# RWKV's group norm inside the recurrence, its output projection entered by halves, and the feed-forward's sums by halves

## The reference, cut to what matters

```python
def swiglu(x, w_in, w_out):
    gate, up = jnp.split(x @ w_in, 2, axis=-1)
    return (jax.nn.silu(gate) * up) @ w_out
# RWKV, after the scan over the tokens has given y (16 heads of 64)
    mean = jnp.mean(y, axis=-1, keepdims=True)
    var = jnp.mean(jnp.square(y - mean), axis=-1, keepdims=True)
    y = ((y - mean) * lax.rsqrt(var + RWKV_LNX_EPS)).reshape(bsz, seq, D_MODEL)
    y = y * lnx_g.astype(f32) + lnx_b.astype(f32)
    bonus = jnp.sum(r_h * k_h * r_k.astype(f32), axis=-1, keepdims=True) * v_h
    y = y + bonus.reshape(bsz, seq, D_MODEL)
    return (y * g.astype(f32)).astype(x.dtype) @ w_o
```

## Time and profile before

| | |
|---|---|
| median of 3 runs | 3061.42 us (3059.08 to 3068.48) |
| the profiled execution | 3060.07 us, its span 3058.2 us |
| mean granted TensorE clock | 0.987 of full |
| TensorE, VectorE, ScalarE, GpSimd busy | 95%, 68%, 46%, 2% |
| recurrence | about 1376 to 1583.5 us |
| from its end to the output projection's first matmul | 1583.5 to 1617 us |
| output projection | 1617 to 1641.8 us |
| moved from and to memory | 471 MB, 154 GB/s over the span |

### The profile page before, as it was taken

The page is one execution under the profiler, slowest core; times in us unless marked ns, Lnnn a source line. Parts: engine busy times, 40 slices in busy tenths (PEclk is TensorE's granted clock), DMA queues, the critical chain, the costliest instruction groups (busy, mean ns, idle before and its releaser), DMA issues.

```text
span 3058.2 us, 43817 instructions
## 1 busy us (share of the span) xinstructions
PE 2915.9 (95%) x17418; PEld 2526.0 (83%) x17418; DVE 2077.7 (68%) x2566; ACT 1420.9 (46%) x1778; POOL 48.5 (2%) x43
## 2 busy tenths in 40 slices
PE   7998999999999999999999999998999999989998
PEld 6887787888888788888977888886887888988887
DVE  5767677776767677677766767766776775565676
ACT  4445545445444544652214445445545444445443
POOL 0000000000000000100000000000000000000000
PEclk9999999999999999999999999999999999999999
DMA  8643565654466566440004665643565656643662
GB/s 234 203 117 125 178 199 154 192 174 126 137 186 192 164 187 176 127 143 3 1 23 145 192 185 166 206 132 115 177 192 160 191 163 179 187 135 123 201 192 83
DMA packets 614845, 471.23 MB, mean 154 GB/s; under 512 B 40545, under 2 KB 572385, under 8 KB 614708
## 3 DMA queue, kind: packets, MB, share of 16 engines
q1 hardware_dynamic: 614084, 467.60, 50.6%
q10 hardware_dynamic: 624, 1.71, 0.2%
HBM read 466.37 MB, written 1.84 MB: 153 GB/s over the span
## 4 chain that ended last, share of the span: by engine, by line
PE 80%; DVE 10%; ACT 6%; issue 2%; DMA 0%; PEldq 0%; SPq 0%; PEld 0%; DVEq 0%; ACTq 0%
PE pair_bank L402 25%; PE pair_bank L403 13%; PE pair_bank L577 11%; PE out_banks L422 6%; PE out_banks L424 6%; PE out_banks L423 6%; DVE low L337 3%; ACT high L333 2%; PE out_banks L577 2%; PE pair_bank L2168 2%; PE pair_bank L2182 1%; PE pair_bank L2180 1%; DVE h L720 1%; DVE y L710 1%; DVE sq_scratch L484 0%
## 5 line engine op out<-in xcount | busy, mean ns | idle before, releaser
L337 DVE TENSOR_TENSOR low<-raw,high 128x3072 fp32r<-128x3072 f32 (+2 forms) x328 | 934.4, 2849 | 589.0 <-ACT high L333 588.2
L402 PE MATMUL pair_bank<-x_parts,high 128*128 128x512 f32 x3520 | 1240.9, 394 | 26.8 <-DVE x_parts L777 21.6
L403 PE MATMUL pair_bank<-x_parts,low 128*128 128x256 f32 x3520 | 985.7, 280 | 0.0
L333 ACT ACTIVATE high<-raw 128x3072 fp32r<-128x3072 f32 (+2 forms) x328 | 774.0, 2360 | 150.2 <-PE out_banks L424 51.7
L402 PEld LDWEIGHTS pair_bank<-x_parts,high 128*128 128x128 f32 x3520 | 661.1, 188 | 185.6 <-issue 27.3
L403 PEld LDWEIGHTS pair_bank<-x_parts,low 128*128 128x128 f32 x3520 | 666.1, 189 | 9.1
L452 ACT ACTIVATE sq_scratch<-pair_bank 128x512 f32<-128x512 f32 x220 | 132.0, 600 | 541.8 <-PE pair_bank L403 541.8
L422 PE MATMUL out_banks<-high,hid_h 128*128 128x512 f32 x880 | 348.2, 396 | 11.4 <-DVE hid_l L493 11.4
L424 PE MATMUL out_banks<-high,hid_l 128*128 128x512 f32 x880 | 347.8, 395 | 0.0
L423 PE MATMUL out_banks<-low,hid_h 128*128 128x512 f32 x880 | 347.7, 395 | 0.0
L454 ACT ACTIVATE silu<-sq_scratch 128x256 f32<-128x256 f32 x220 | 91.9, 418 | 351.7 <-DVE sq_scratch L484 351.7
(11 more groups left out here) (363 smaller groups left out, 3115.8 us busy)
## 6 DMA issues: line engine op xcount, KB each, us to landing
raw<-in_ffn_w_in_dram SPq DMA_DIRECT2D x352, 512.0 KB
raw<-in_ffn_w_out_dram SPq DMA_DIRECT2D x176, 512.0 KB
raw<-in_ffn_w_dram SPq DMA_DIRECT2D x132, 512.0 KB
raw<-in_w_in_dram SPq DMA_DIRECT2D x32, 1024.0 KB
raw<-in_gla_w_in_dram SPq DMA_DIRECT2D x12, 1024.0 KB
raw<-in_rwkv_w_rkv_dram SPq DMA_DIRECT2D x12, 1024.0 KB
raw<-in_swa_w_qkv_dram SPq DMA_DIRECT2D x10, 1024.0 KB
raw<-in_swa_w_o_dram SPq DMA_DIRECT2D x8, 1024.0 KB
```

The source lines that it names most:

```text
L333: nc.scalar.activation(high[u % SPLIT][:, lo:w], raw[u % RAW][:, lo:w], ACT.Copy).then_inc(high_ready, count)
L337: nc.vector.tensor_tensor(low[u % SPLIT][:, lo:w], raw[u % RAW][:, lo:w], high[u % SPLIT][:, lo:w].bitcast(F32), ALU.subtract).then_inc(we ...
L402: nc.tensor.matmul(o, H[:, w], x_parts[:, k, :], start=(k == 0), stop=False)
L403: last = nc.tensor.matmul(o[:, 0:SEQ], L[:, w], xh[:, k, :], start=False, stop=(k == KB - 1))
```

## The change

Seven parts, all in one diff:

- **Group norm in the recurrence.** The two tail steps and the lone turn are gone. For pair c: VectorE sums and scales the mean at step 0 of round c+2, sums and scales the variance at step 2, and takes the reciprocal at step 5; ScalarE takes the root at step 3; GpSimd multiplies the values by the bonus and adds the bias, subtracts the mean, squares, multiplies by the reciprocal and the gain, and adds, seven operations of 256 columns. Pair 7 is done by VectorE after the recurrence and beside the projection (GpSimd does its bonus and bias). The result stands in the values' own place.
- **Gate product in the ninth round**, one of four parts behind each of steps 0 to 3, and at step 4 the transposes of columns 0 to 511. VectorE and ScalarE gate and split that half at steps 3 and 4.
- **Output projection by halves.** It starts with blocks 0 to 3. VectorE ends pair 7 and gates the second half at chunk 0, TensorE transposes it between the two groups of chunk 1, and its parts are split at chunk 1.
- **Loads.** SyncE loads gain and bias rows into free ends of `raw` slots right behind the projection's weights, then waits until pair 6 is joined, and loads g2 into that pair's place; the next feed-forward's first weights stand behind this in its queue.
- **Unit 0 of each feed-forward**: all 16 high products first, when the high weights are there, then the 16 low ones.
- **Sums by halves**: add and scale 256 columns of gate, then of up; the silu may start after the first.
- **Crossings before a feed-forward**: VectorE splits unit 0's weights after the x parts and not before; at the program's start ScalarE copies x before it splits weights and takes roots, and TensorE runs 8 keep-warm products behind the transposes.

Semaphores of the recurrence's grams are merged into fewer, with the same waits.

```diff
@@ ffn_pe @@
+                elif q == 0:
+                    pe.wait_ge(high_ready, u + 1)
                 else:
                     pe.wait_ge(weights_split, u + 1 + UNROLL * turn)
...
+                    for n in range(2 if q == 0 else 0):
+                        for k in range(KB):
+                            if n == 0:
+                                x_wait(pe, st, k)
+                            w, o = block(n, k)
+                            nc.tensor.matmul(o, H[:, w], x_parts[:, k, :], start=(k == 0), stop=False)
+                    if q == 0:
+                        pe.wait_ge(weights_split, u + 1)
                     for n in range(2):
                         for k in range(KB):
...
+                            if q > 0:
+                                nc.tensor.matmul(o, H[:, w], x_parts[:, k, :], start=(k == 0), stop=False)
                             last = nc.tensor.matmul(o[:, 0:SEQ], L[:, w], xh[:, k, :], start=False, stop=(k == KB - 1))
@@ ffn_dve @@
-                    nc.vector.tensor_tensor(sums[:, :, :], lows[:, :, :], halves[:, :, 0:SEQ],
-                                            ALU.add).then_inc(sums_made, 1)
...
+                    for n in range(2):
+                        nc.vector.tensor_tensor(sums[:, n, :], lows[:, n, :], halves[:, n, 0:SEQ], ALU.add).then_inc(sums_made, 1)
+                        dve.wait_ge(sums_made, 3 * g + n + 1 + 3 * UNROLL * turn)
+                        nc.vector.tensor_tensor(sums[:, n, :], sums[:, n, :], scale_rows, ALU.mult).then_inc(
+                            sums_ready if n == 0 else sums_made, 1)
@@ cross_act, program start @@
-            if st.at == 0:
-                split_high(act, 0, words(0))
...
                                          scale=gain_columns[st.turned0 % 2][:, k:k + 1]).then_inc(x_high, 1)
+                if st.at == 0:
+                    split_high(act, 0, words(0))
+                    pre_root(0)
                 if st.scales_later:
                     pre_root(1)
+                if st.at == 0 and split_early(stages[1]):
+                    split_early_high(act, stages[1])
@@ cross_dve: behind the x_low loop @@
                 if st.scales_later:
+                    if splits_first(st):
+                        split_low(dve, next_unit(st.at - 1), words(next_unit(st.at - 1)))
+                    if st.at == 0:
+                        split_low(dve, 0, words(0))
@@ cross_pe @@
+            if st.at == 0:
+                keep_warm(WARM_OPEN)
@@ core_pe, end of a step @@
+                if not here and n < 4:
+                    gate_pe(e, pe, n // 2, n % 2)
+                elif not here and n == 4:
+                    turn_half_pe(e, pe, 0)
@@ core_act, end of a step @@
+                if n == 3 and c >= 2:
+                    root_act(e, act, c - 2)
+                if n == 4 and c == R_PAIRS:
+                    turn_half_act(e, act, 0)
@@ core_dve, end of a step @@
+                if c >= 2:
+                    if n == 0:
+                        mean_dve(e, dve, c - 2)
+                    elif n == 2:
+                        var_dve(e, dve, c - 2)
+                    elif n == 5:
+                        rstd_dve(e, dve, c - 2)
+                if c == R_PAIRS and n == 3:
+                    dve.wait_ge(S("rw_normed"), R_PAIRS // 2)
+                    gate_dve(e, dve, 0)
+                elif c == R_PAIRS and n == 4:
+                    turn_half_dve(e, dve, 0)
+        last_pair = R_PAIRS - 1
+        mean_dve(e, dve, last_pair)
...
+        var_dve(e, dve, last_pair)
@@ new @@
+    def core_pool(e, pool, st):
...
+        for c in range(R_PAIRS):
+            pool.wait_ge(S("rw_stored"), NT * (c + 1))
+            heads = by_token(e, c).rearrange("p t (h d) -> p t h d", d=R_HD)
+            own(g_.tensor_tensor(heads, heads, bonus(e.mix)[:, :, 2 * c:2 * c + 2].unsqueeze(3).to_broadcast([P, NT, 2, R_HD]), ALU.mult))
+            g_.tensor_tensor(by_token(e, c), by_token(e, c), each_tile(lnx_b(e), c), ALU.add).then_inc(S("rw_biased"), 1)
+            if c == R_PAIRS - 1:
+                continue
+            pool.wait_ge(S("rw_mean"), c + 1)
+            own(g_.tensor_tensor(groups(e, c), groups(e, c), along(four_of(mean(e.mix), c), R_HD), ALU.subtract))
+            g_.tensor_tensor(squared(e), groups(e, c), groups(e, c), ALU.mult).then_inc(S("rw_squared"), 1)
+            pool.wait_ge(S("rw_squared"), c + 1)
+            pool.wait_ge(S("rw_rstd"), c + 1)
+            own(g_.tensor_tensor(groups(e, c), groups(e, c), along(four_of(var(e.mix), c), R_HD), ALU.mult))
+            own(g_.tensor_tensor(tiles_of(e, c), tiles_of(e, c), each_tile(lnx_g(e), c), ALU.mult))
+            pool.wait_ge(S("rw_biased"), c + 1)
+            g_.tensor_tensor(by_token(e, c), by_token(e, c), tiles_of(e, c), ALU.add).then_inc(S("rw_normed"), 1)
...
+    def out_wait(e, pe, k):
+        if k == 0:
+            pe.wait_ge(e.named("rw_stored"), NT * R_PAIRS)
+        pe.wait_ge(e.named("rw_turned_low"), 2 if k < KB // 2 else 4)
+
+    def out_pe(e, pe, st, c, x):
+        if (c, x) == (1, 0):
+            turn_half_pe(e, pe, 1)
...
+    def out_dve(e, dve, st, c, emptied):
+        vv, last = e.nc.vector, R_PAIRS - 1
+        if (c, emptied) == (0, False):
+            rstd_dve(e, dve, last)
...
+            gate_dve(e, dve, 1)
+        elif (c, emptied) == (1, False):
+            turn_half_dve(e, dve, 1)
+
+    def out_sp(e, sp, st, c):
+        if c == len(st.chunks) - 1:
+            for dst, row in ((lnx_g(e), io["rwkv_lnx_g"][0]), (lnx_b(e), io["rwkv_lnx_b"][0])):
+                sp.dma_start(dst, spread(row)).then_inc(e.named("rw_affine_loaded"), 16)
+            sp.wait_ge(e.named("rw_joined"), 2 * NL * (R_PAIRS - 1))
+            sp.dma_start(g2a(e.mix), io["rwkv_g2"][0, 0:P, :]).then_inc(e.named("rw_gate_loaded"), 16)
+            sp.dma_start(g2b(e.mix, slice(0, 32)), io["rwkv_g2"][0, P:GR, :]).then_inc(e.named("rw_gate_loaded"), 16)
@@ stages @@
-              step(core_pe, core_act, core_dve), after_step(), step(g_pe, root_act, affine_dve), step(dve=gate_dve, warm=15),
-              Stage("turn", kb=KB, src=result),
-              Stage("proj", chunks=half_rows(io["rwkv_w_o"][0]), feature_major=False, dest="out", evac=None),
+              core_step(),
+              Stage("proj", chunks=half_rows(io["rwkv_w_o"][0]), feature_major=False, dest="out", evac=None, x_wait=out_wait,
+                    flows=True, beside_pe=out_pe, beside_act=out_act, beside_dve=out_dve, beside_sp=out_sp),
```

205 lines of the change are left out of this document (123 added, 82 removed).

## The result

The changed kernel takes 3024.61 us (median of 4 runs, 3019.41 to 3027.26) against 3062.53 us for the kernel before: a ratio of 0.9869, 95% interval 0.9849 to 0.9888. Faster, as forecast, but by 38 us and not by 29. The quotient of the two medians alone is 0.9876, inside the interval. On the scale of the 3061.42 us ahead of the prediction, 0.9869 gives 3021.3 us, just under the range's lower end of 3023, and 0.9876 gives 3023.5 us, just above it: the result lies at that end either way, 8 to 11 us from the forecast of 3032. The profiled execution took 3019.41 us (span 3017.4), 40.7 us less than that of before. It is also the fastest of the four.

A forecast was written before the change was run, and what follows sets the result against it. TensorE, with work in 95% of the span, bounds the kernel, so time is to be had only where its order breaks, as in the tail. -29.0 + 2.5 - 3.3 - 1.8 + 2.8 = -28.8 us gave 3032 us, range 3023 to 3043.

The forecast's parts named there:

- part B: Recurrence: norm work added on VectorE and GpSimd costs +2.5 us, bounds 0 and 9.
- 0.4 us lost per pair: Recurrence: VectorE's mask products at steps 0 and 1, each late by up to 0.6 us beside GpSimd, lose this much.
- Part A: Tail after the recurrence: steps removed, gate products between the last pair's links, projection by halves; -29.0 us.
- waits up to 0.8 us: Output projection: TensorE asks for the second half at 1597.3 us, VectorE has it at 1597.8 us.
- the rule of the ports: Trainium skill: ports shared by VectorE and GpSimd lock for a whole instruction, also for VectorE operations with two SBUF inputs.
- Part C: Program's opening: x copies before ScalarE's weight splits and roots let units 0 to 2 start earlier; -3.3 us.
- part D: Feed-forward sums by halves: 0.18 us at each of ten waits for hid_l, -1.8 us, bounds 0 and -5.
- E: Unit 0's high products first: +0.55 us after each of five mixers, zero between feed-forwards; +2.8 us, bounds 0 and +5.
- Rival 3: Better than costed: B and E in slack, opening at its best; 3025 us, chance 0.14.
- Rivals 1 and 4: Ports hold VectorE at recurrence's critical steps, 3041 us, chance 0.14; VectorE waits in order for GpSimd's square, 3085 us, 0.03.
- Rival 2: Projection: second half late, TensorE stands at its transposes and loses 3 to 6 us; 3037 us, chance 0.07.
- rival 5: Next feed-forward's weights come late behind SP's new wait, TensorE stands 20 us or more; 3055 us, chance 0.02.

The follow-up runs named there:

- entered whole: Changed kernel with the second half's eight transposes ahead of the output projection, not behind its 36th matmul: 3036.04 us, ratio 0.9916, RWKV stage +11.5 us.
- gates behind: Changed kernel with the second half's gate products behind the last pair's output, not between its links: 3026.33 us, ratio 0.9888, RWKV stage +2.08 us.
- next execution: The changed kernel itself, unaltered, timed and profiled a second time: 3022.61 us, ratio 0.9868.

## Why the prediction was right and wrong

The mechanism of the gain was right, and the time came out below the range. The step that failed is part B's "0.4 us lost per pair", counted through to the end; three smaller terms erred the same way, and some of the difference is chance.

- **What bounds it** held: the tail, where TensorE had no useful work, gave 30.4 of some 38 us.
- **Part A** (forecast -29.0) was right in kind and short by 1.4 us. From the last inverse's end to the projection's start it is 15.15 us, for 16.0; the rest takes 23.2 us, for 23.7. The term "waits up to 0.8 us" for the second half was zero. That both covers count, "entered whole" (+11.5) and "gates behind" (+2.1) show.
- **Part B** (forecast +2.5) measured 0.0: the recurrence's first and last pair products are 193.7 us apart in both traces (1377.1 to 1570.8, 1369.4 to 1563.1). The failed step is "0.4 us lost per pair". VectorE does lose time beside GpSimd, 0.7 us a round and so more than the prediction said, and its mask products are longer than 0.42 us on average, which the prediction named as a sign of being wrong. But the loss never reaches TensorE. At the first join it goes into VectorE's wait (1.13 us before, 0.82 after). At the second, the late mask products and the small operations of step 0 together take up VectorE's wait of 0.41 us and 0.46 us of TensorE's slack of 0.74 us. The prediction had both of these numbers, from the earlier trace rows, and held them against the small operations alone; the loss by the ports it counted in full. A delay is to be carried to the next wait, of its own engine and then of the engine that it serves, before it is counted. The prediction's sum without the rule of the ports (0.5 us) came nearer than the one with it (2.5 to 9), though VectorE was held as the rule says.
- **Part C** (-3.3, bounds -1 and -5) measured -5.1 and -4.8 from the start to the first mixer, some 0.6 of it part D's. Unit 1 started 5.8 us early (28.48, 22.67), unit 2 4.9 us (37.51, 32.59). The chain was the one named (ScalarE's early split, VectorE's), but it ended at 22.6 us, not at 23.2 to 24.7. The clock lost in the gap, which set the bound of -1, had no effect on the end.
- **Parts D and E** are one chain that the prediction split wrongly. E's loss after a mixer was costed at +0.85 and relieved by 0.3 for the earlier silu; measured +0.8, unrelieved. The relief stands in the steps behind the row sums: -4.47 us for -1.8, of which the halves have 3.0 by the run with whole sums, and 0.6 more at the start; the last 1.5 us of those steps were not told apart. Part D's own term, the ten waits for hid_l, measured 2.0 us (11.4 to 9.4) for 1.8; its size came from "1.66 us where 1.89 were", which is 0.23 us and not the 0.18 that the sum took. Together D and E came to -0.6 us, for +1.0; 1.3 us of that is the one step at half clock before.
- **The range** failed on what is in no part: the four untouched mixers, -4.76 us in the profiled pair, -1.70 in the next execution. The sum was made against one execution of before (3060.07 us), whose clock in these stretches was a draw of its own, and the range was built from the costs of the edits alone. Of the 12.0 us, A accounts for 1.4, B for 2.5, C for 1.8 (with 0.6 of D's), D and E for 1.6 (1.3 of it by the clock of one step), and the untouched mixers for 4.8. So some 6 us belong to the parts and some 6 us to the clock of one step and to stretches that the change doesn't touch. Against the second execution the miss is 8.8 us, as it is by the medians. The errors of the parts alone would have given 3026 us, inside the range.
- **Rivals.** Rival 3, better than costed at 3025 us, came nearest; its reasons for B and C held, that for E did not. Rivals 1 and 4 are mechanisms that exist: the first was kept away by where GpSimd's operations lie, the second by 5.1 us of slack. Rival 2 has no wait to show, and rival 5 none either: the next feed-forward's units kept their pace (its row-sum step is the +0.8 us of the others).

## What to carry to other kernels

Work for an idle engine and small pieces of work on a busy one may be put into a pipelined loop at nothing, if each delay ends in a wait that its engine has anyway; where that slack is used up (here 5.1 us at the in-order wait, 1.13 us ahead of step 0's join, 0.74 us behind step 1's, none ahead of step 4's) the rest of the delay is paid in every round, with the clock on top. A consumer with several chunks can start on half its input, and when products wait for parts that come one by one, the part belongs in the outer loop. A forecast made against single executions should carry the scatter of the stretches that it doesn't touch.

## What was not expected of the hardware

- The same instructions in the same order take 108.1 to 111.3 us (attention mixer) and 315.4 to 321.5 us (hybrid mixer) from one execution or kernel to the next, with a granted clock of 0.81 or 0.86 in the same stretch. In the opening the same sixteen matmuls took 3.92 or 5.56 us behind keep-warm products. On this the Trainium skill (TensorE: Matmul & The Clock Gate, section "What's actually happening") says that the number of slow matmuls at a kernel's start varies between runs; the opening agrees, and the mixers show it far from the start too.
- A GpSimd operation of 128x256 with two inputs took 0.61 to 0.81 us on average by line and 0.97 us for one line (L2436, whose longest, 2.67 us, lay beside VectorE's split of 2.53 us, itself 2.29 alone).
- VectorE's operations with a PSUM input kept their 0.41 us beside GpSimd, where those with two SBUF inputs went from 0.74 to 1.81 us for two.
